# A scan's last group reordered on all engines, and one block of attention scores moved behind a tile of values

## The chip, the cores and the metric

The kernel runs on one core of a Trainium2 chip. A core has five engines with instruction streams of their own: TensorE (matmuls, called PE in the profile; its weight loads are PEld), VectorE (DVE), ScalarE (ACT), GpSimd (POOL) and SyncE (SP, which here only issues DMAs). They wait for one another by semaphores that are raised when an instruction ends. The metric is the device time of one launch in microseconds, lower is better.

## The reference, cut to what matters

The program is a two-layer network (convolution mixer, dilated attention and two SwiGLU layers) followed by a second two-layer network: a bidirectional state-space mixer (SSD) and a bidirectional gated linear attention mixer (GLA). All of it is float32, for 512 positions and 1024 channels. The change touches the end of the first and the start of the second of the last two:

```python
def ssd_scan(xh, dt, a, bm, cm):            # 4 chunks of 128 positions, 8 groups of 4 heads
    def step(state, inp):
        cum = jnp.cumsum(lac, axis=1)
        decay = jnp.exp(jnp.where(causal, cum[:, :, None] - cum[:, None], -jnp.inf))
        cb = jnp.einsum('blgn,bsgn->blsg', cc, bc)
        y = jnp.einsum('blsgr,bsgrp->blgrp', cb[..., None] * decay, xdt)      # within the chunk
        y = y + jnp.einsum('blgn,bgrpn->blgrp', cc, state) * jnp.exp(cum)[..., None]
...
def ssd_mixer(...):
    y = ssd_scan(forward) + rev(ssd_scan(backward)) + xh * d_skip
    y = y * silu(z)
    y = rmsnorm(y per group of 256 channels, gnorm)      # root of the mean square
    return y @ w_out                                     # 2048 x 1024
...
def gla_scan(q, k, v, lg):                   # 4 heads, chunks of 64
        qg = qc * jnp.exp(cum); kg = kc * jnp.exp(-cum)
        att = jnp.where(causal, jnp.einsum('blhk,bshk->bhls', qg, kg), 0.0)
        o = jnp.einsum('bhls,bshv->blhv', att, vc) + jnp.einsum('blhk,bhkv->blhv', qg, s)
```

## The kernel before, in words

Each large product is done as three passes of TensorE over split float32 numbers: high weights by high data, high weights by low data and low weights by high data. A unit is one block of weights, 128 x 2048 numbers. For each unit SyncE loads `raw`, ScalarE writes `whi` (L741), GpSimd (once, in the last group, VectorE) writes `wlo` (L652), and TensorE uses both. There are two buffers of each, taken in turn by even and odd units, so ScalarE may write the `whi` of unit n only when TensorE has marked the end of unit n-2: `high()` waits for `mm` to reach `2 * (n - 1)`, two marks for each unit.

The scan runs over eight groups of heads with four chunks each; chunk number n counts to 31, and the last group, 7, has n = 28 to 31. Nothing is planned at run time: the order on each engine is the order in which its code is written, and each waits at its own semaphores. For each n:

- ScalarE adds the bias of both directions to decay rows that a DMA brought (`biased`, L1046), VectorE takes the smaller of the two (`least`, L1705), and ScalarE takes the exponential (`exponential`, L1063).
- GpSimd multiplies the masked products of C and B with the step sizes, once for each direction (L680), adds the two (L683) and multiplies the sum with the exponential (L686). The result `MT` is the weight of the chunk.
- TensorE computes what the state carries in (L2537) and the chunk's own part (L2541): `chunk_out`.
- VectorE sums the parts (`collect`), and multiplies two chunks at a time with the gate (`gate`, L1745).

At the end of a group ScalarE sums squares (`squares`, L1085), VectorE scales the sum (L1696), ScalarE takes the root (L1089), VectorE inverts it and scales the whole group with it (L1698, L1700), and TensorE transposes the result (`turn_out`, L2519). ScalarE keeps it in `sY` (`turned_out`, L1094) and splits it into `sHi` (`y_hi`, L761), and VectorE makes `sLo` (`y_low`, L1750). These 16 tiles are the data of the output product (units 132 to 139, `U_SSD_OUT` and on).

In the last group TensorE fills its waits with the output product of the first two output tiles, k = 0 (unit 132) and k = 1 (unit 133): `out_high` (L2570), `out_low_weight` (L2575) and `out_low` (L2581). The tiles j = 0 to 13 of the data come from earlier groups; 14 and 15 are the last group's own. Only after j = 14 and 15 of k = 0 is unit 132 marked as done. Then the third output tile follows, unit 134, from L2641. ScalarE's order after the last group is: wait for the residual sum that VectorE makes from output tile 0 (L1435), write its high part and its square (L761, L772), and only then write the `whi` of unit 134:

```python
for i in range(4):
    for s in range(2):
        if i or s:
            ahead(U_SSD_OUT, i, s)
        split_square(5, 2 * i + s)
```

At the start of GLA, TensorE computes the values of head 0 in tiles of 128 positions (`projected`; a half of one tile is 12 matmuls of 512 columns). The scores of head 0 (`scores(0)`, L2721 and L2724) are placed between the two tiles of one call, and they wait until VectorE has multiplied queries and keys with their decays (L1906).

Of the kernel before, what the change touches and what calls it, by code (L numbers as in the profile page):

```python
# [14 lines left out]
P = 128  # L15
# [10 lines left out]
HPG = 4  # L26
# [158 lines left out]
def build(nc, A, out, stop=None):  # L185
# [8 lines left out]
    with ExitStack() as ctx:  # L194
# [5 lines left out]
        def S(name):  # L200
            if name not in sems:
                sems[name] = ctx.enter_context(nc.semaphore(name))
            return sems[name]
# [191 lines left out]
        def coupling(n):  # L395

            return m_ssd[("P0", "P1")[n % 2]][:, :]

        FB = bank[2]
        DTH = 2 * SSD_HEADS  # L400

# [224 lines left out]
        def _(pool):  # L626
# [43 lines left out]
            def coupled(n):  # L670

                g, c = n // NT, n % NT
                if c == 0:
                    pool.wait_ge(S("cb_ready"), 2 * g + 2)
                if n >= 2:
                    pool.wait_ge(S("mt_ready"), n - 1)
                if n:
                    pool.wait_ge(S("p_ready"), n)
                for d, dst in enumerate((coupling(n), acc[:, :])):
                    pool.tensor_tensor(v3(dst, HPG), bc(heads("dt", c, d, g), P), rep(m_ssd["CB"][:, SEQ * d + P * c:SEQ * d + P * (c + 1)], HPG),  # L680
                                       ALU.mult).then_inc(S("p_part"), 1)
                pool.wait_ge(S("p_part"), 2 * n + 2)
                pool.tensor_tensor(coupling(n), coupling(n), acc[:, :], ALU.add).then_inc(S("p_ready"), 1)  # L683
                pool.wait_ge(S("p_ready"), n + 1)
                pool.wait_ge(S("ex_ready"), n + 1)
                pool.tensor_tensor(weights(n), weights(n), coupling(n), ALU.mult).then_inc(S("mt_ready"), 1)  # L686
# [45 lines left out]
        def _(act):  # L732
# [236 lines left out]
            if on("ssd"):  # L969
# [179 lines left out]
                def last_group(g):  # L1149

                    for k in range(4):
                        y_hi(k)
                    exponential(NT * g)
                    biased(NT * g + 1)
                    turned_out(g - 1, 0)
                    exponential(NT * g + 1)
                    biased(NT * g + 2)
                    turned_out(g - 1, 1)
                    y_hi(4)
                    exponential(NT * g + 2)  # L1160
                    biased(NT * g + 3)
                    for k in range(5, 8):
                        y_hi(k)
                    exponential(NT * g + 3)
                    z_silu(g, 0)
                    z_silu(g, 1)
                    for k in range(8, 11):
                        y_hi(k)
                    unit_high(U_SSD_OUT + 1)
                    for k in range(11, 14):  # L1170
                        y_hi(k)
                    squares(g, 0)
                    squares(g, 1)
                    group_root(g)
                    for e in range(2):
                        turned_out(g, e)
                        y_hi(14 + e)
# [218 lines left out]
        def _(dve):  # L1396
# [224 lines left out]
            if on("ssd"):  # L1621
# [144 lines left out]
                def last_group(g):  # L1766
# [7 lines left out]
                    least(n + 1)  # L1774
                    keep_z(g)
                    y_low(0)
                    least(n + 2)
                    for k in range(1, 3):
                        y_low(k)
                    collect(g, 0)  # L1780
                    least(n + 3)
                    for k in range(3, 5):
                        y_low(k)
                    collect(g, 1)
# [1 line left out]
                    collect(g, 2)  # L1786
                    collect(g, 3)
                    gate(g, 1)
                    for k in range(5, 7):
                        y_low(k)  # L1790
                    normalise(g)
                    for k in range(7, IT):
                        y_low(k)

                def group(g):
# [256 lines left out]
        def _(pe):  # L2052
# [358 lines left out]
            if on("ssd"):  # L2411
# [172 lines left out]
                def last_group(g):  # L2584
# [9 lines left out]
                    chunk_out(g, 1)  # L2594
                    unit(U_SSD_OUT)
                    pe.wait_ge(S("sy_kept"), 2 * g)
                    for ks in (range(0, 4), range(4, 6)):
                        out_high(0, ks)
                        out_low_weight(0, ks)
                        if ks.start == 0:  # L2600
                            chunk_out(g, 2)
                    out_low(0, range(0, 4))
                    chunk_out(g, 3)
                    for ks in (range(6, 8), range(8, 14)):
                        out_high(0, ks)
                        out_low_weight(0, ks)
                    pe.wait_ge(w_hi, U_SSD_OUT + 2)
                    pe.wait_ge(S("ex_ready"), NT * SSD_GROUPS)
                    out_high(1, range(14))
                    for e in range(2):  # L2610
                        turn_out(g, e)
                    out_low(0, range(4, 14))
                    out_low(1, range(14))
                    for k in range(2):
                        if k:
                            unit(U_SSD_OUT + 1)
                            out_low_weight(1, range(14))
                        for j in range(14, IT):
                            out_high(k, (j,))
                            out_low_weight(k, (j,))  # L2620
                            mark(out_low(k, (j,)))
# [33 lines left out]
            if on("gla"):  # L2655
# [141 lines left out]
                gates(0)  # L2797
                projected("v", 0, 0, 0)
                projected("v", 0, 0, 1)
                projected("v", 0, 1, 0, lambda: scores(0))  # L2800
                projected("v", 0, 1, 1, lambda: keys(0))
                for h in range(GLA_HEADS):
                    head(h)
# [107 lines left out]
```

## Time and profile before

| | us |
|---|---|
| median of 3 runs | 2059.2 (2058.72 to 2060.91) |
| the profiled execution | 2057.88 |
| its span in the trace | 2055.9 |
| TensorE busy in the span | 2024.0 (98%) |
| VectorE, ScalarE, GpSimd busy | 896.8, 840.8, 1032.9 |

The profiled execution is 1.98 us longer than its span, which is what lies around the first and last instruction, and 1.3 us below the median. Busy times of TensorE are of pipelined matmuls: a record of one matmul of 512 columns is 0.39 us long, though the next starts 0.23 us after it. A row of a timeline gives start, duration, engine, line, operation, what it writes and reads, shape and count; in brackets stands how long the engine was idle before it and what ended that. "issue" means that the profile shows nothing for which the engine waited.

### The profile page before, as it was taken

To read this page: it belongs to the slowest core of one execution; us is meant where nothing else is said; L and a number is where in the kernel's file an instruction comes from. 1 tells how busy PE (TensorE), PEld (TensorE's weight loads), DVE (VectorE), ACT (ScalarE), POOL (GpSimd) and SP (SyncE) were. 2 spreads that over 40 slices of the span, in tenths; PEclk is the share of its full clock that TensorE was granted. 3 is DMA by queue.
4 is the path that set the end of the run, shared out by engine and by line. 5 is a ranking of instruction groups with operands and counts; after the bars stand their busy time and mean duration, and the time that the engine had idled before them with its cause. 6 is when DMAs were issued, how large, how long until landed. Compare 5 with 4: busy or idle time off the path is not lost.

```text
span 2055.9 us, 25781 instructions
## 1 busy us (share of the span) xinstructions
PE 2024.0 (98%) x9884; PEld 1654.1 (80%) x9884; DVE 896.8 (44%) x1411; ACT 840.8 (41%) x1341; POOL 1032.9 (50%) x855
## 2 busy tenths in 40 slices
PE   9999999999999999999999999999999999999998
PEld 7888888888877777888888778988887876677787
DVE  3184433322144435334322388778875215443331
ACT  4123222222244443222222377677774325544543
POOL 4455544545532224544545468788885441323242
PEclk9999999999999999999999999999999999999999
DMA  5223233223433312333233334434432321112131
GB/s 169 97 87 113 83 103 103 84 84 97 126 91 93 92 42 82 103 103 102 84 89 101 102 105 123 122 104 114 133 103 62 105 84 62 60 63 81 43 103 62
DMA packets 259365, 193.28 MB, mean 94 GB/s; under 512 B 9459, under 2 KB 247335, under 8 KB 259256
## 3 DMA queue, kind: packets, MB, share of 16 engines
q1 hardware_dynamic: 256188, 190.67, 30.9%
q8 instruction: 77, 1.26, 0.3%
q10 hardware_dynamic: 3068, 1.09, 0.2%
q14 instruction: 32, 0.26, 0.0%
HBM read 189.46 MB, written 2.27 MB: 93 GB/s over the span
## 4 chain that ended last, share of the span: by engine, by line
PE 38%; issue 35%; POOL 21%; DVE 2%; ACT 2%; DMA 1%; POOLq 0%; SPq 0%; ACTq 0%; DVEq 0%
POOL wlo L652 21%; PE bank L2058 11%; PE bank L2060 11%; PE bank L2059 11%; PE bank L2541 1%; PE bank L2537 1%; PE bank L2505 1%; DMA raw<-in_conv_w_in 0%; DVE xc L1668 0%; ACT whi L741 0%; DVE hLo L1971 0%; DMA rows<-cums 0%; PE bank L2519 0%; PE bank L2493 0%; PE bank L2477 0%
## 5 line engine op out<-in xcount | busy, mean ns | idle before, releaser
L652 POOL TENSOR_TENSOR wlo<-raw,whi 128x512 fp32r<-128x512 f32 (+1 forms) x664 | 842.4, 1299 | 942.7 <-ACT whi L741 942.7
L2058 PE MATMUL bank<-hHi,whi 128*128 128x512 f32 (+1 forms) x1392 | 548.4, 394 | 3.8 <-DVE qk L1554 1.5
L2060 PE MATMUL bank<-hHi,wlo 128*128 128x512 f32 (+1 forms) x1392 | 540.7, 388 | 0.0
L2059 PE MATMUL bank<-hLo,whi 128*128 128x512 f32 (+1 forms) x1392 | 540.4, 388 | 0.0
L741 ACT ACTIVATE whi<-raw 128x2048 fp32r<-128x2048 f32 (+1 forms) x167 | 301.8, 1807 | 476.0 <-PE bank L2060 473.0
L2058 PEld LDWEIGHTS bank<-hHi,whi 128*128 128x128 f32 x1392 | 261.4, 188 | 63.2 <-issue 6.6
L2060 PEld LDWEIGHTS bank<-hHi,wlo 128*128 128x128 f32 x1392 | 261.3, 188 | 54.8
L2059 PEld LDWEIGHTS bank<-hLo,whi 128*128 128x128 f32 x1392 | 261.5, 188 | 53.2 <-issue 1.2
L2058 PE MATMUL bank<-whi,hHi 128*128 128x256 f32 (+1 forms) x640 | 219.4, 343 | 2.2 <-POOL wlo L652 1.8
L2060 PE MATMUL bank<-whi,hLo 128*128 128x256 f32 (+1 forms) x640 | 208.5, 326 | 0.0
L2059 PE MATMUL bank<-wlo,hHi 128*128 128x256 f32 (+1 forms) x640 | 208.3, 326 | 0.0
L1435 DVE TENSOR_TENSOR xT<-xT,bank 128x512 f32<-128x512 f32 x47 | 32.3, 687 | 303.3 <-PE bank L2060 290.4
L2058 PEld LDWEIGHTS bank<-whi,hHi 128*128 128x128 f32 x640 | 121.6, 190 | 20.2 <-issue 8.2
L2059 PEld LDWEIGHTS bank<-wlo,hHi 128*128 128x128 f32 x640 | 121.7, 190 | 13.7 <-issue 4.5
L2060 PEld LDWEIGHTS bank<-whi,hLo 128*128 128x128 f32 x640 | 121.5, 190 | 10.4
L1668 DVE SCALAR_TENSOR_TENSOR xc<-bank,vecT,xc 128x510 f32<-128x510 f32 (+1 forms) x96 | 72.0, 749 | 3.7 <-ACT xc L987 0.3
L2060 PE MATMUL bank<-f0aHi,wlo 128*128 128x512 f32 x176 | 68.5, 389 | 0.0
L2060 PE MATMUL bank<-f1aHi,wlo 128*128 128x512 f32 x176 | 68.5, 389 | 0.0
L2058 PE MATMUL bank<-f0aHi,whi 128*128 128x512 f32 x176 | 68.5, 389 | 0.0
L2059 PE MATMUL bank<-f0aLo,whi 128*128 128x512 f32 x176 | 68.5, 389 | 0.0
L2058 PE MATMUL bank<-f1aHi,whi 128*128 128x512 f32 x176 | 68.5, 389 | 0.0
L2059 PE MATMUL bank<-f1aLo,whi 128*128 128x512 f32 x176 | 68.5, 389 | 0.0
(387 smaller groups left out, 2930.7 us busy)
## 6 DMA issues: line engine op xcount, KB each, us to landing
raw<-in_ssd_w_in SPq DMA_DIRECT2D x48, 512.0 KB, 4.8
raw<-in_ffn_w_gate SPq DMA_DIRECT2D x44, 512.0 KB, 4.7
raw<-in_ffn_w_up SPq DMA_DIRECT2D x44, 512.0 KB, 4.7
raw<-in_gla_w_in SPq DMA_DIRECT2D x40, 512.0 KB, 4.6
rows<-cums SPq DMA_DIRECT2D x64, 256.0 KB, 5.4
raw<-in_ffn_w_down SPq DMA_DIRECT2D x32, 384.0 KB, 3.6
raw<-in_attn_w_qkv SPq DMA_DIRECT2D x24, 512.0 KB, 4.5
raw<-in_conv_w_in SPq DMA_DIRECT2D x23, 512.0 KB, 4.4
```

Source lines behind the costliest of these rows:

```text
L652: ins = pool.tensor_tensor(wlo[s][:, part], raw[s][:, part], whi[s][:, part].bitcast(F32), ALU.subtract)
L741: act.activation(whi[s][:, 0:w], raw[s][:, 0:w], ACT.Copy).then_inc(w_hi, 1)
L1435: tt(x, x, bank[b][:, :], ALU.add).then_inc(res_done, 1)
L1668: ins = stt3(y[:, to:to + w], u[:, frm:frm + w], tapcol(j, ct), y[:, to:to + w], ALU.mult, ALU.add)
L2058: pe.matmul(dst, hi1, hi2, start=first, stop=False)
L2059: pe.matmul(dst, hi1, lo2, start=False, stop=False)
L2060: return pe.matmul(dst, lo1, hi2, start=False, stop=last)
L2505: ins = pe.matmul(bank[4 + step][:, 256 * d:256 * d + 256], bt[:, P * c:P * (c + 1)], xw_buf(step, d), start=True, stop=True)
L2537: pe.matmul(carried_bank(c, d), conv_tile(g, 3)[:, P * c:P * (c + 1)], m["stt"][:, SEQ * step + 256 * d:SEQ * step + 256 * d + 256], start ...
L2541: ins = pe.matmul(intra_bank(c)[:, 64 * h:64 * h + 64], weights(n)[:, P * h:P * (h + 1)], xt[:, 256 * c + 64 * h:256 * c + 64 * h + 64], s ...
```

## The change

`last_coupling(n)` names a buffer for n = 30 and 31 only. For these two chunks GpSimd no longer makes the product of the second direction; VectorE makes it, into `t32`, between `y_low(0)` and `least(30)`, and raises a semaphore that GpSimd waits for before its addition. The order of VectorE, ScalarE and TensorE in the last group changes as below. ScalarE gets one activation more, a square root of one column of ones ahead of the squares. In GLA the scores of head 0 stand behind both tiles of values rather than between them.

```diff
+        def last_coupling(n):
+            return t32[n % 2][:, :] if n >= NT * SSD_GROUPS - 2 else None
+        def coupled_aside(n):
+            return S("x_in3"), 16 + n - (NT * SSD_GROUPS - 3)
...                                   (GpSimd, coupled)
+                other = last_coupling(n)
                 for d, dst in enumerate((coupling(n), acc[:, :])):
+                    if d and other is not None:
+                        break
                     pool.tensor_tensor(v3(dst, HPG), ...
-                pool.wait_ge(S("p_part"), 2 * n + 2)
-                pool.tensor_tensor(coupling(n), coupling(n), acc[:, :], ALU.add).then_inc(S("p_ready"), 1)
+                if other is None:
+                    pool.wait_ge(S("p_part"), 2 * n + 2)
+                else:
+                    pool.wait_ge(S("p_part"), n + NT * SSD_GROUPS - 1)
+                    pool.wait_ge(*coupled_aside(n))
+                pool.tensor_tensor(coupling(n), coupling(n), acc[:, :] if other is None else other, ALU.add).then_inc(S("p_ready"), 1)
...                                   (ScalarE, last_group)
                     exponential(NT * g + 1)
+                    turned_out(g - 1, 1)
                     biased(NT * g + 2)
-                    turned_out(g - 1, 1)
                     y_hi(4)
...
                     exponential(NT * g + 3)
+                    for k in range(8, 11):
+                        y_hi(k)
                     z_silu(g, 0)
                     z_silu(g, 1)
-                    for k in range(8, 11):
+                    for k in range(11, 14):
                         y_hi(k)
                     unit_high(U_SSD_OUT + 1)
-                    for k in range(11, 14):
-                        y_hi(k)
+                    act.activation(m["hcol"][:, 2:3], ones[:, 0:1], ACT.Sqrt)
                     squares(g, 0)
...                                   (VectorE, last_group)
                     y_low(0)
+                    for c in (2, 3):
+                        tt(v3(last_coupling(n + c), HPG), bc(heads("dt", c, 1, g), P), rep(m["CB"][:, SEQ + P * c:SEQ + P * (c + 1)], HPG),
+                           ALU.mult).then_inc(coupled_aside(n + c)[0], 1)
                     least(n + 2)
                     for k in range(1, 3):
                         y_low(k)
+                    least(n + 3)
                     collect(g, 0)
-                    least(n + 3)
...
-                    for k in range(5, 7):
-                        y_low(k)
+                    y_low(5)
                     normalise(g)
-                    for k in range(7, IT):
+                    for k in range(6, IT):
                         y_low(k)
...                                   (TensorE, last_group)
-                    for ks in (range(0, 4), range(4, 6)):
-                        out_high(0, ks)
-                        out_low_weight(0, ks)
-                        if ks.start == 0:
-                            chunk_out(g, 2)
-                    out_low(0, range(0, 4))
+                    out_high(0, range(5))
+                    out_low_weight(0, range(5))
+                    chunk_out(g, 2)
+                    out_low(0, range(3))
+                    for j in range(5, 8):
+                        out_high(0, (j,))
+                        out_low_weight(0, (j,))
                     chunk_out(g, 3)
-                    for ks in (range(6, 8), range(8, 14)):
-                        out_high(0, ks)
-                        out_low_weight(0, ks)
+                    out_high(0, range(8, 14))
+                    out_low_weight(0, range(8, 14))
                     pe.wait_ge(w_hi, U_SSD_OUT + 2)
                     pe.wait_ge(S("ex_ready"), NT * SSD_GROUPS)
                     out_high(1, range(14))
                     for e in range(2):
                         turn_out(g, e)
-                    out_low(0, range(4, 14))
+                    unit(U_SSD_OUT + 1)
+                    out_low_weight(1, range(14))
+                    out_low(0, range(3, 14))
                     out_low(1, range(14))
                     for k in range(2):
-                        if k:
-                            unit(U_SSD_OUT + 1)
-                            out_low_weight(1, range(14))
                         for j in range(14, IT):
                             out_high(k, (j,))
                             out_low_weight(k, (j,))
...                                   (TensorE, GLA)
-                projected("v", 0, 1, 0, lambda: scores(0))
+                projected("v", 0, 1, 0)
+                scores(0)
                 projected("v", 0, 1, 1, lambda: keys(0))
```

## Rows read from the trace of the kernel before

**Rows 1.** The page, part 1: busy time, share and instructions.
```profile
PE 2024.0 (98%) x9884; PEld 1654.1 (80%) x9884; DVE 896.8 (44%) x1411; ACT 840.8 (41%) x1341; POOL 1032.9 (50%) x855
```
**Rows 2.** Waits of TensorE: total us, times, longest.
```profile
PE bank L2721 <- DVE kg L1906: 2.3, 1, 2.3
PE bank L2519 <- DVE szs L1700: 1.8, 1, 1.8
```
**Rows 3.** Timeline of TensorE, the scan's last group and the output product.
```profile
1538.73 2.04 PE L2570 MATMUL bank<-sHi,whi 128*128 128x512 f32 x4 [1.53 <-issue]
...
1542.06 1.03 PE L2537 MATMUL bank<-stt,xC 128*128 128x256 f32 x4
...
1558.83 1.09 PE L2519 MATMUL bank<-ident,szs 128*128 128x128 f32 x8 [1.76 <-DVE szs L1700]
1559.68 7.06 PE L2581 MATMUL bank<-sLo,whi 128*128 128x512 f32 x24
...
1567.94 3.33 PE L2575 MATMUL bank<-sHi,wlo 128*128 128x512 f32 x14
...
1572.47 0.39 PE L2641 MATMUL bank<-sHi,whi 128*128 128x512 f32 x1
```
**Rows 4.** Timelines of TensorE and VectorE around head 0's scores.
```profile
1704.21 0.39 PE L2060 MATMUL bank<-whi,hLo 128*128 128x512 f32 x1
1706.93 1.13 PE L2721 MATMUL bank<-gO,kg 128*128 128x128 f32 x8 [2.34 <-DVE kg L1906]
...
1706.10 0.69 DVE L1906 TENSOR_TENSOR kg<-gQK,kg 128x512 f32<-128x512 f32 x1
1710.41 0.42 DVE L1915 TENSOR_TENSOR diff<-diff,gdec 128x256 f32<-128x256 f32 x1 [3.62 <-PE bank L2724]
```
**Rows 5.** Timeline of ScalarE, the same stretch.
```profile
1535.62 1.28 ACT L1046 ACTIVATE rows<-rows,ncum 128x128 f32<-128x128 f32 x4 [2.40 <-DMA rows<-cums]
...
1543.64 0.60 ACT L1063 ACTIVATE MT<-bank 128x512 f32<-128x512 f32 x1
1544.26 1.28 ACT L1073 ACT_TABLE_LOAD   x1
1545.55 0.72 ACT L1073 ACTIVATE szs<-szs 128x256 f32<-128x256 f32 x2
...
1553.61 0.42 ACT L1085 ACTIVATE back<-szs 128x256 f32<-128x256 f32 x1 [0.75 <-DVE szs L1745]
...
1554.48 0.19 ACT L1085 ACTIVATION_READ_ACCUMULATOR back<-szs 128x1 f32 x1
...
1570.09 1.90 ACT L741 ACTIVATE whi<-raw 128x2048 fp32r<-128x2048 f32 x1
```
**Rows 6.** Timeline of VectorE, the same stretch.
```profile
1533.28 1.65 DVE L1750 TENSOR_TENSOR sLo<-sY,sHi 128x512 fp32r<-128x512 f32 x1
1538.06 0.70 DVE L1705 TENSOR_TENSOR bank<-bank,rows 128x512 f32<-128x512 f32 x1 [3.14 <-ACT bank L1046]
...
1553.50 3.48 DVE L1750 TENSOR_TENSOR sLo<-sY,sHi 128x512 fp32r<-128x512 f32 x2
1556.91 0.16 DVE L1696 TENSOR_SCALAR stat<-stat 128x4 f32<-128x4 f32 x1
...
1558.69 5.50 DVE L1750 TENSOR_TENSOR sLo<-sY,sHi 128x512 fp32r<-128x512 f32 x9
```
**Rows 7.** Timeline of GpSimd, the same stretch.
```profile
1542.49 1.03 POOL L680 TENSOR_TENSOR acc<-dt,CB 128x512 f32<-128x512 f32 x1
...
1550.50 5.93 POOL L652 TENSOR_TENSOR wlo<-raw,whi 128x512 fp32r<-128x512 f32 x4 [3.47 <-ACT whi L741]
1572.07 10.95 POOL L652 TENSOR_TENSOR wlo<-raw,whi 128x512 fp32r<-128x512 f32 x8 [15.63 <-ACT whi L741]
```
**Rows 8.** Windows: PE, PEld, DVE, ACT, POOL busy, granted clock, DMA.
```profile
1539.20:1539.70 0.50, 0.50 (x2) 0.33 (x2) 0.50 (x1) 0.50 (x2) 0.19 (x1) 0.50 1.09 315
...
1706.90:1708.00 1.10, 1.06 (x9) 0.98 (x9) 0.00 (x0) 0.00 (x0) 0.00 (x0) 1.00 0.00 0
```

## The prediction

> **What bounds the kernel now.** I read part 1 of the page first: TensorE is busy 2024.0 of 2055.9 us [rows 1], so all that this change can win is idle time or slowed matmuls of TensorE. The list of TensorE's waits then says where such time lies: the longest single ones are 2.3 us before the scores of head 0 and 1.8 us before the last group's transposes [rows 2]. The timeline of TensorE through the last group shows what surrounds these: a gap of 1.53 us before the first output matmuls (called "issue", but it ends with the `turned_out` of ScalarE), then the 1.76 us before the transposes, then 24 low passes that span 7.06 us, where 24 at full rate would span 5.6 (24 x 0.2265, and 0.16 by which a record outlasts its step) [rows 3]. The full rate is one matmul of 512 columns each 0.2265 us: from 1567.94 to 1572.47 there are 20 (14 of L2575, then six of k = 1) [rows 3]. Last I read the other engines' timelines to see which chain ends each of these waits. The sum below follows two points: T, the start of the last transposes (1558.83 before), and R, the start of the third output tile (1572.47 before) [rows 3]. What TensorE gains ahead of T is worth nothing by itself, as it waits there in any case.
>
> **The scores of head 0.** The last matmul before them starts at 1704.21, so the next could start at 1704.44; the scores start at 1706.93, and the cause, the last product of VectorE, ends at 1706.10 + 0.69 = 1706.79 [rows 4]. The loss is 2.49 us. Moved behind one half tile more (12 matmuls, 12 x 0.2265 = 2.72 us), the scores would start at 1707.16, which leaves 0.23 us to spare. The chain that ends at 1706.79 starts from gate products that are not moved. Behind the scores, the transposes of the keys now come 2.7 us after them rather than 5.4, and VectorE needs four products of 0.42 us in between [rows 4], about 1.7 us: still covered. ScalarE's `whi` of the next unit gets free earlier, not later. Gain: **2.5 us**, between 0 (if a new wait appears at once) and 2.5.
>
> **T, the last transposes.** Their chain is ScalarE's and VectorE's. It starts with decay rows that a DMA lands at 1535.6 [rows 5]; nothing in the change moves that load, since SyncE's order is the same and what it waits for (the exponentials of chunks 28 and 29) is not moved.
> - `turned_out(6, 1)` goes into the 2.40 us in which ScalarE waits for those rows [rows 5]. TensorE's gap of 1.53 us goes, but `y_hi(4)` becomes needed at once and is made only behind the eight bias activations that start at 1535.62, near 1538.6, so some 0.6 us stay. All this is ahead of T.
> - VectorE's two products go into its idle 3.14 us ahead of `least(30)` [rows 6]. The trace has no such product of two SBUF operands of this size in this spot. The neighbour `y_low(0)` took 1.65 us while GpSimd worked, and nine others took 5.50 us, 0.61 each, while it was idle [rows 6]. Two products are so 1.2 to 3.3 us; I take 3.2, by the neighbour. That ends at about 1538.1 and costs `least(30)` nothing to 0.2 us. GpSimd sheds two products of 1.03 us [rows 7], so the last two weights of chunks are ready sooner; ahead of T as well.
> - `exponential(31)` stood at 1543.64 behind `least(31)`, itself behind `collect(0)`. With `least(31)` first, ScalarE runs through: about 0.4 us earlier, 1543.2.
> - The silus' table load, four silus, six `y_hi` and the `whi` of unit 133 keep their total; only their order changes.
> - The new root brings a table load of 1.28 us and a 0.2 us activation ahead of the squares, +1.5 us. A table load costs no more than its length here: the one at 1544.26 was followed by a silu at 1545.55 [rows 5]. Against it, the squares waited 0.75 us for the gate and will no more [rows 5].
> The last sum of squares ended at 1554.48 + 0.19 = 1554.67 [rows 5]; now 1554.67 - 0.4 + 1.5 - 0.75 = 1555.0. Before, that was not the bound: VectorE was inside two `y_low` until 1556.98 [rows 6], and the table load ran beside it. With one `y_low` fewer it comes free near 1555.1. From L1696 to T it took 1558.83 - 1556.91 = 1.92 us [rows 3, 6], with GpSimd idle (it had ended at 1550.50 + 5.93 = 1556.43) [rows 7]. That gives T = 1557.0 at the least. But `whi` of unit 133 now ends at about 1551.5, a micro-second late against before (GpSimd started behind it at 1550.50), so GpSimd is in its four passes until about 1557.4, and the scaling of the group (L1700) falls into them. Beside GpSimd a `y_low` took 1.74 us instead of 0.61 [rows 6]: so up to 1.5 us more, one pass (5.93 / 4) [rows 7]. T lies in 1557.0 to 1558.6; I take 1557.8, the middle, since a pass is met at any point. TensorE reaches the place near 1555.1 and idles 2.7 us.
>
> The Trainium skill (SBUF — State Buffer, section "SBUF: two separate sides") has a rule for it: VectorE and GpSimd take a shared port pair as an exclusive lock for a whole instruction, and the loser blocks. The rows at 1.74 against 0.61 us agree. The Trainium skill (ScalarE: Activation LUTs, section "What ACT_TABLE_LOAD costs") speaks against the root ahead of the squares: it adds a drain of 1.38 us to each load. By that T would be 1.4 us later; the row at 1545.55 shows a start 0.01 us behind the load, so I go by the row.
>
> **From T to R.** Before: T to R took 13.64 us: the transposes 0.85, 50 matmuls at 0.2265 (11.3), and 1.5 lost to `y_low` [rows 3]. After, the 14 low-weight matmuls of k = 1 stand first, and one low pass more is left: 14 + 11 + 14 + 6 = 45 matmuls up to and with j = 15 of k = 0, then only six of k = 1. VectorE's ten `y_low` behind the scaling (0.61 each) are ahead of TensorE throughout, so the 1.5 us are won.
> But the third output tile needs the `whi` of unit 134, and that chain is short of cover now. Its buffer is unit 132's, free with the last matmul of k = 0. Behind this come VectorE's residual sum, ScalarE's high part and square, and then L741 at 1570.09 for 1.90 us, so 1571.99 [rows 5]. Counted from 1567.94, when the first matmul behind k = 0 started [rows 3], this is 4.05 us, and some 0.06 to TensorE: 4.11. Before, 20 matmuls (4.53 us) stood in between, so nothing waited, with 0.4 us to spare. Now there are six (1.36 us): TensorE idles 2.75 us. So R = T + 0.85 + 45 x 0.2265 + 4.11 = T + 15.15 = 1572.95, 0.5 us later than before. The bounds of T give -0.3 to +1.3 us.
> Further on, GpSimd makes the `wlo` of units 134 and 135 in 10.95 us from the end of `whi` [rows 7]; TensorE needs the second 48 matmuls (10.9 us) behind R. Before, ScalarE wrote `whi` 0.48 us ahead of R, now 0.06: up to 0.25 us of waiting. SSD in all: +0.75 us (-0.3 to +1.6).
>
> **TensorE's clock.** Once in this stretch it fell: behind the idle 1.53 us the granted clock is 0.50, the 1.2 GHz level [rows 8], and the eight matmuls from 1538.73 to 1542.06 took 3.33 us instead of 1.81 [rows 3], 1.5 us lost. Behind the idle 2.34 us at the scores it stayed 1.00 [rows 4, 8]. The change makes two idle stretches of 2.7 us at T and before R, longer than both, and TensorE sets the pace behind each. Cost: 0 to 3.0 us. I take 0, by the row nearest in length. The fall that goes with the old gap lay ahead of T and wins nothing.
>
> **Sum.** -2.5 + 0.5 + 0.25 = -1.75 us against the profiled 2057.88, so 2056.1; the median of the runs lies 1.3 above that execution, so I put it at 2059.2 - 1.75, about **2057.5**. That is 0.09% and, with less than about 0.2% (4.1 us) not to be told from no change here, "the same".
>
> **Rivals.**
> - *The clock falls behind one or both new idle stretches.* For it: they are longer than any in this region, and a shorter one already did it. Against: 2.34 us did not. One fall gives 2059.0, two give 2060.5, slower than before; it decides as soon as the two together cost more than 1.75 us. Chance 0.32.
> - *The third tile's weights are covered anyhow*, and the order on TensorE pays in full: R = T + 0.85 + 51 x 0.2265 = T + 12.4 = 1570.2, 2.3 us earlier, with the scores -4.8: 2054.4. Against: the wait on unit 132's marks stands in the code. Chance 0.09.
> - *VectorE's products do not fit into its idle time.* They would delay `least(30)`, and by ScalarE's unbroken chain T, by up to 1.5 us: 2058 to 2059. Against: 3.14 us of room. Chance 0.1.
> - *The scores' move does not do what it says*, as the wait comes back at the keys or the increments: 2.5 us less gain, 2060.0. Against: each needs less than it has. Chance 0.06.
> The forecast itself has 0.43, with a range of its own of 2056.3 to 2059.1. With all of them the range is 2055.0 to 2061.0. Faster by over 0.2% is the second rival and little else: 0.09. Slower needs two falls and a late T, or a part of this mechanism that I have not seen: 0.06. The same: 0.85.
>
> **What the profile of the changed kernel would show.** No wait at L2721. At L2570 no wait of 1.5 us. At L2519 a wait of 2 to 3 us for L1700, which ends 0 to 1.8 us earlier than before. At L2641 a new wait of about 2.7 us for L741: if it is not there, the forecast is wrong. L1696 would follow the squares at once, and the L2581 rows would run at 0.23 us each. Windows behind both waits tell by their granted clock whether the first rival holds. A time below 2055 or above 2061 would say that I have missed a chain.

## The result and the profile after

The changed kernel takes 2062.18 us (median of 20 runs, 2059.79 to 2066.46) against 2058.77 us before (20 runs): ratio 1.0014, 95% interval 1.0008 to 1.0020. It is slower by 0.14%. The forecast was 2057.5 us in a range of 2055.0 to 2061.0, so the time lies above the range, and the sign is the other one. The profiled execution took 2061.72 us, with a span of 2059.8 us.

First the longest waits of TensorE after the change (total us, times, longest; they answer to [rows 2]):

```profile
PE bank L2537 <- DVE szs L1716: 2.9, 1, 2.9
PE bank L2658 <- ACT whi L756: 2.6, 1, 2.6
...
PE bank L2749 <- DVE gO L1933: 1.8, 1, 1.8
PE bank L2588 <- ACT sHi L776: 1.8, 2, 1.3
```

Lines have shifted: L2537 is the last transposes (L2519 before), L2588, L2593 and L2599 are the output passes (L2570, L2575, L2581), L2658 is the third output tile (L2641), L2749 the transposes of the keys (L2732), L2738 the scores (L2721). On the other engines L1716, L1712 and L1933 are the scaling of the group, the step on its four sums and the span products, that is the products ahead of the keys' transposes (L1700, L1696, L1915); L756 and L660 write `whi` and `wlo` (L741, L652). The wait at the scores is gone, a new one of 1.8 us stands at the keys, the wait at T has grown, and the forecast wait of 2.6 us before the third tile is there.

TensorE's timeline, changed kernel, for [rows 3]:

```profile
1548.28 1.83 PE L2588 MATMUL bank<-sHi,whi 128*128 128x512 f32 x3 [1.26 <-ACT sHi L776]
1549.91 2.22 PE L2593 MATMUL bank<-sHi,wlo 128*128 128x512 f32 x6
1551.97 3.33 PE L2588 MATMUL bank<-sHi,whi 128*128 128x512 f32 x14
1558.24 1.97 PE L2537 MATMUL bank<-ident,szs 128*128 128x128 f32 x8 [2.94 <-DVE szs L1716]
1559.86 4.25 PE L2593 MATMUL bank<-sHi,wlo 128*128 128x512 f32 x14
1563.94 5.83 PE L2599 MATMUL bank<-sLo,whi 128*128 128x512 f32 x25
...
1575.06 0.65 PE L2658 MATMUL bank<-sHi,whi 128*128 128x512 f32 x1 [2.57 <-ACT whi L756]
1575.51 0.63 PE L2659 MATMUL bank<-sLo,whi 128*128 128x512 f32 x1
```

The 25 low passes span 5.83 us, which is the full rate: the 1.5 us that VectorE's `y_low` cost are won. But the eight transposes take 1.62 us to the next row instead of 0.85, the 14 passes behind them 4.08 instead of 3.17, and behind the third tile's wait matmuls start 0.43 us apart. The windows (PE, PEld, DVE, ACT, POOL busy, granted clock, DMA) show why, for [rows 8]:

```profile
1559.00:1560.00 1.00, 1.00 (x7) 1.00 (x5) 1.00 (x3) 0.61 (x1) 0.00 (x0) 0.50 1.01 304
...
1576.00:1577.00 1.00, 1.00 (x4) 0.81 (x3) 1.00 (x2) 1.00 (x2) 1.00 (x2) 0.50 0.00 0
```

The clock is at 0.50, the 1.2 GHz level, behind both idle stretches. VectorE's timeline, for [rows 6]:

```profile
1552.96 1.78 DVE L1766 TENSOR_TENSOR sLo<-sY,sHi 128x512 fp32r<-128x512 f32 x1
1554.69 1.21 DVE L1712 TENSOR_SCALAR stat<-stat 128x4 f32<-128x4 f32 x1
1556.18 0.18 DVE L1714 RECIPROCAL stat<-stat 128x4 f32<-128x4 f32 x1 [0.27 <-ACT stat L1104]
1556.39 1.79 DVE L1716 TENSOR_TENSOR szs<-szs,stat 128x1024 f32<-128x1024 f32 x1
```

and GpSimd's beside it, for [rows 7]:

```profile
1551.20 5.90 POOL L660 TENSOR_TENSOR wlo<-raw,whi 128x512 fp32r<-128x512 f32 x4 [6.10 <-ACT whi L756]
```

Even the step on four columns (L1712) takes 1.21 us instead of 0.16 while GpSimd is at its four passes, and the scaling 1.79 instead of 1.22. Last, the keys: TensorE, then VectorE, then GpSimd, and ScalarE ahead of it.

```profile
1711.47 1.05 PE L2738 MATMUL bank<-gO,kg 128*128 128x128 f32 x8
...
1719.61 1.09 PE L2749 MATMUL bank<-ident,diff 128*128 128x128 f32 x8 [1.84 <-DVE gO L1933]
```

```profile
1714.86 0.43 DVE L1933 TENSOR_TENSOR diff<-diff,gdec 128x256 f32<-128x256 f32 x1 [3.76 <-PE bank L2741]
1715.20 1.51 DVE L1933 TENSOR_TENSOR gO<-gO,gdec 128x256 f32<-128x256 f32 x1
1716.64 1.51 DVE L1933 TENSOR_TENSOR diff<-diff,gdec 128x256 f32<-128x256 f32 x1
1718.07 1.48 DVE L1933 TENSOR_TENSOR gO<-gO,gdec 128x256 f32<-128x256 f32 x1
```

```profile
1713.71 5.56 POOL L660 TENSOR_TENSOR wlo<-raw,whi 128x512 fp32r<-128x512 f32 x4 [13.41 <-ACT whi L756]
```

```profile
1711.73 1.91 ACT L756 ACTIVATE whi<-raw 128x2048 fp32r<-128x2048 f32 x1 [1.47 <-PE bank L2078]
```

The same two in the kernel before:

```profile
1713.41 1.92 ACT L741 ACTIVATE whi<-raw 128x2048 fp32r<-128x2048 f32 x1 [7.47 <-PE bank L2060]
1715.41 5.01 POOL L652 TENSOR_TENSOR wlo<-raw,whi 128x512 fp32r<-128x512 f32 x4 [19.41 <-ACT whi L741]
```

Three of the four span products, which took 0.42 us each [rows 4], now take 1.5 us. The 12 matmuls that now run ahead of the scores let ScalarE write its next `whi` earlier: it starts 0.26 us behind the start of the scores (1711.47), where it started 6.48 us behind it before (1706.93). With it GpSimd's low part now starts ahead of the span products; before, it began at 1715.41, when they had ended at 1711.8.

All profiles are put together by a few marks on TensorE: F, the first matmul of chunk 28; T; R; Q, the fourth output tile; S, the scores; G, the gate products of head 1 (the first such row behind S). Each column is a difference of two starts in a timeline, in us:

| kernel | F to T | T to R | R to Q | Q to G | S to G | G to end |
|---|---|---|---|---|---|---|
| before | 25.48 | 13.64 | 10.88 | 136.23 | 12.65 | 336.32 |
| changed | 25.33 | 16.82 | 12.60 | 135.72 | 11.91 | 336.42 |
| difference | -0.15 | +3.18 | +1.72 | -0.51 | | +0.10 |

With 0.44 us less ahead of F this makes 3.9 us, the difference of the spans. Each kernel has one profile, so these are differences of two single executions.

### The profile page after: what moved, and what is told of

The parts are those of the page before. It is cut to its first block, busy times and chain, and to the rows that moved or that the text cites. A ratio compares the mean times of both kernels' runs of the same rounds, so it can differ in the third digit from the quotient of the medians.

```text
span 2059.8 us, 25784 instructions
## 1 busy us (share of the span) xinstructions
PE 2025.8 (98%) x9884; PEld 1655.7 (80%) x9884; DVE 902.9 (44%) x1413; ACT 840.8 (41%) x1342; POOL 1031.5 (50%) x853
## 3 DMA queue, kind: packets, MB, share of 16 engines
q8 instruction: 77, 1.26, 0.3%
## 4 chain that ended last, share of the span: by engine, by line
PE 38%; issue 35%; POOL 21%; ACT 2%; DVE 2%; DMA 1%; POOLq 0%; SPq 0%; ACTq 0%; DVEq 0%
POOL wlo L660 21%; PE bank L2076 11%; PE bank L2078 11%; PE bank L2077 11%; PE bank L2559 1%; PE bank L2555 1%; PE bank L2523 1%; DMA raw<-in_conv_w_in 0%; DVE xc L1684 0%; ACT whi L756 0%; DVE hLo L1989 0%; DMA rows<-cums 0%; ACT sHi L776 0%; PE bank L2537 0%; PE bank L2511 0%
## 5 line engine op out<-in xcount | busy, mean ns | idle before, releaser
L660 POOL TENSOR_TENSOR wlo<-raw,whi 128x512 fp32r<-128x512 f32 (+1 forms) x664 | 842.7, 1300 | 947.1 <-ACT whi L756 947.1
L756 ACT ACTIVATE whi<-raw 128x2048 fp32r<-128x2048 f32 (+1 forms) x167 | 301.7, 1807 | 469.8 <-PE bank L2078 466.9
```

What stands on the lines that cost most here:

```text
L660: ins = pool.tensor_tensor(wlo[s][:, part], raw[s][:, part], whi[s][:, part].bitcast(F32), ALU.subtract)
L756: act.activation(whi[s][:, 0:w], raw[s][:, 0:w], ACT.Copy).then_inc(w_hi, 1)
```

## The experiments

Each was timed in five rounds beside the kernel before on the same chip; medians and ratios are against those runs. Where two kernels of this list are compared in time, it is by their ratios to the kernel before. Each has one profile.

**1. The scores' move alone.**
```diff
-                projected("v", 0, 1, 0, lambda: scores(0))
+                projected("v", 0, 1, 0)
+                scores(0)
```


> The kernel before with the scores of head 0 moved behind both tiles of values, nothing else. Theory A (the earlier release of the weights lets GpSimd's low parts run beside VectorE's four span products, which then take 1.5 us each instead of 0.42, so the keys wait about 1.8 us): the wait at the scores (2.3 us) goes, one of 1.8 us comes at the keys, and the time falls by 0.5 us only. Theory B (the move pays in full and what the changed kernel shows there is a result of its other edits): 2.5 us less.

Measured: 2057.15 us against 2059.8, ratio 0.9991 (0.9982 to 1.0000). S to G is 11.91 us, Q to G 135.72, exactly as in the changed kernel, and the waits of TensorE have

```profile
PE bank L2732 <- DVE gO L1915: 1.8, 1, 1.8
```

So the wait at the keys comes with the move, not with the other edits. In the profile it wins 0.51 us; the runs show 1.9 us, with an interval that holds both. Two profiles of kernels with the old order (experiments 2 and 4) can explain the rest: there the clock fell behind the scores' wait and S to G was 14.18 us, not 12.65. Against those two the move wins 2.1 us from Q to G. How often the kernel before meets this was not measured.

**2. The tail alone.** The kernel before, with the low-weight passes of k = 1 moved.
```diff
+                    unit(U_SSD_OUT + 1)
+                    out_low_weight(1, range(14))
                     out_low(0, range(4, 14))
...
-                        if k:
-                            unit(U_SSD_OUT + 1)
-                            out_low_weight(1, range(14))
```


> The kernel before with one edit: the 14 low-weight passes of k = 1 stand right behind the last transposes rather than between k = 0 and k = 1. Theory A (the third output tile's high weights lose their cover): TensorE idles about 2.7 us before it, R moves from T + 13.6 to T + 15.15, so 1.5 us slower, and 3.1 us slower if the clock falls behind the idle time. Theory B (the loss of the changed kernel comes from the scan's chain on ScalarE and VectorE, not from the tail): no slower than before, or 1.4 us faster because the low passes no longer wait for VectorE.

Measured: 2062.29 us against 2059.8, ratio 1.0012 (1.0003 to 1.0021). T to R is 15.05 us with the clock at full rate throughout. The forecast's formula gives 14.93 here, since this kernel has one low pass less behind T than the changed one (44 matmuls, not 45). This one reordering is by itself as slow as the whole change, though in this profile no clock fell behind R.

```profile
PE bank L2640 <- ACT whi L741: 2.6, 1, 2.6
```

**3. The changed kernel with the old tail.**
```diff
-                    unit(U_SSD_OUT + 1)
-                    out_low_weight(1, range(14))
...
+                        if k:
+                            unit(U_SSD_OUT + 1)
+                            out_low_weight(1, range(14))
```


> The changed kernel with its tail put back (the low-weight passes of k = 1 again between k = 0 and k = 1). Theory A: no wait for the third tile's high weights (2.6 us) and no slowed clock behind it (1.6 us); the low passes wait for VectorE again for up to 1.5 us: 3 to 4.4 us faster than the changed kernel, so about the time of before or 1 us below. Theory B: at most 1 us from the changed kernel.

Measured: 2058.25 us against 2059.8, ratio 0.9993 (0.9984 to 1.0002), so 4.3 us below the changed kernel's 1.0014. No wait at the third tile, R to Q 10.88. T to R is 15.33, as the clock still fell behind T. TensorE idled 3.6 us there, longer than in the changed kernel, since its clock had stayed up ahead of T in this execution and it came earlier:

```profile
1558.75 1.97 PE L2537 MATMUL bank<-ident,szs 128*128 128x128 f32 x8 [3.65 <-DVE szs L1716]
```

**4. The changed kernel with the old place of the scores.**
```diff
-                projected("v", 0, 1, 0)
-                scores(0)
+                projected("v", 0, 1, 0, lambda: scores(0))
```


> The changed kernel with the scores of head 0 put back between the two tiles. Theory A: the 1.8 us at the keys go and the 2.3 us at the scores come back, 0.5 us slower than the changed kernel. Theory B (the move pays in full): 2.5 us slower.

Measured: 2062.87 us against 2059.8, ratio 1.0017 (1.0008 to 1.0026): 0.6 us above the changed kernel's ratio, less than the intervals can tell. In this execution the clock stayed up behind T, and T to R is 15.26: the changed kernel's 16.82 less one fall. The idle time at T was shorter too, as the clock had been at 0.50 ahead of T and TensorE came later:

```profile
1558.79 1.09 PE L2537 MATMUL bank<-ident,szs 128*128 128x128 f32 x8 [1.61 <-DVE szs L1716]
```

**5. The idle stretches filled.** Both got 11 matmuls into an unread bank.
```diff
                     out_high(1, range(14))
+                    pe.wait_ge(S("sz_ready"), NT * SSD_GROUPS)
+                    for j in range(11):
+                        pe.matmul(bank[1][:, :], m_ssd2["sHi"][:, P * j:P * (j + 1)], tile(m_ssd2["sHi"], 0), start=True, stop=True)
...                                 (and the same ahead of the wait for unit 134's high weights)
```


> The changed kernel with 11 matmuls of 512 columns more in each of its two new idle stretches (ahead of the last transposes and ahead of the third output tile), into a bank that nothing reads. They add 2 x 2.5 us of work to TensorE and no use. Theory A (behind the idle stretches the clock falls to half, and that is a part of the loss): T to R is 15.1 to 15.3 us and R to the fourth tile 10.9 us in every execution, as the clock stays at 1.00, and the time is 1.5 to 3 us below the changed kernel in spite of the added work. Theory B (the slow clock is not tied to the idle time): not faster than the changed kernel, or slower.

Measured: 2059.2 us against 2059.43, ratio 0.9998 (0.9989 to 1.0007): 3.3 us below the changed kernel with 5 us of useless work more. The two intervals do not overlap. T to R is 15.23 and R to Q 11.01, and no window from T to Q is below 1.00:

```profile
1562.00:1566.00 4.00, 4.00 (x21) 3.35 (x20) 4.00 (x7) 2.54 (x4) 0.00 (x0) 1.00 0.84 245
...
1577.00:1580.00 3.00, 3.00 (x15) 2.45 (x14) 2.72 (x2) 2.58 (x3) 3.00 (x3) 1.00 0.00 0
```

So theory A holds: the clock was lost to the idle time. The work put in costs nothing, as it fits into time in which TensorE waited. In the changed kernel's profile the slow clock cost 3.4 us behind 5.5 us of idle time.

**6. The third tile's weights first.**
```diff
+                ahead(U_SSD_OUT, 0, 1)
                 for i in range(4):
                     for s in range(2):
-                        if i or s:
+                        if i:
                             ahead(U_SSD_OUT, i, s)
                         split_square(5, 2 * i + s)
```


> The changed kernel, but ScalarE writes the high weights of the third output tile's unit before the high part and square of the residual rather than behind them. Theory A (the wait at R is for exactly this chain: residual sum, high part, square, weights): the weights come about 2.0 us earlier, the wait at the third tile shrinks from 2.6 to about 0.7 us, no fall of the clock behind it; 2 to 3.5 us faster than the changed kernel, about the time of before. Theory B (something else paces this place): within 0.5 us of the changed kernel.

Measured: 2059.52 us against 2059.43, ratio 0.9997 (0.9988 to 1.0006), 3.5 us below the changed kernel. The wait at the third tile is 0.7 us, and behind it the clock stayed up. T to R is 15.04 with one fall behind T. The fourth tile now waits 0.3 us for GpSimd (R to Q 11.48): the next link of the chain shows.

**7. The scores' move, with the weights behind the keys.**
```diff
-                value_piece(0, 1, 0)
                 turned_keys(0)
+                value_piece(0, 1, 0)
                 value_piece(0, 1, 1)
```


> The kernel before with the scores of head 0 behind both tiles, and ScalarE's high weights of the unit that follows placed behind its two copies of the turned keys, so that GpSimd's low parts don't run beside VectorE's span products. Theory A (the keys wait because both run at once): the span products take 0.42 us each, no wait at the keys, 2 us faster than with the move alone (2.5 us below before, 4 where the clock used to fall behind the scores' wait). Theory B (the span products are slow for another reason): still 1.5 us each, same time as the move alone.

Measured: 2055.57 us against 2059.43, ratio 0.9985 (0.9976 to 0.9994). VectorE's timeline has the span products at their old length, and there is no wait at the keys; S to G is 10.29 us, 1.62 less than with the move alone. The runs show 1.2 us less than with the move alone, with intervals that overlap.

```profile
1710.45 0.42 DVE L1915 TENSOR_TENSOR gO<-gO,gdec 128x256 f32<-128x256 f32 x1
1710.79 0.42 DVE L1915 TENSOR_TENSOR diff<-diff,gdec 128x256 f32<-128x256 f32 x1
1711.12 0.42 DVE L1915 TENSOR_TENSOR gO<-gO,gdec 128x256 f32<-128x256 f32 x1
```

**8. A first attempt at all of it.** The old tail, edits 6 and 7, and GpSimd held back:
```diff
                     pool.wait_ge(w_lo, U_SSD_OUT + 1)
+                    pool.wait_ge(S("sy_scaled"), SSD_GROUPS)
                     unit_low(U_SSD_OUT + 1)
```


> The changed kernel with four edits: the old tail on TensorE, the third tile's high weights ahead of the residual's high part, the GLA weights behind the turned keys, and GpSimd's low part of unit 133 held until VectorE has scaled the last group. Theory A: no wait at the third tile, the scaling of the group takes 1.2 us and L1712 0.2 us, T 1.5 us earlier than in the changed kernel, no wait at the keys: 5 us below before (2.5 from the scores, 2 to 3 from T). Theory B (T is paced by ScalarE's chain and the tail does not matter): 2.5 us below before.

Measured: 2061.69 us against 2059.43, ratio 1.0009 (1.0000 to 1.0018): a miss. T came 1.75 us earlier than in the changed kernel (F to T 23.58), as expected. But GpSimd's passes now ran beside the ten `y_low`, on which the old tail waits:

```profile
1557.56 1.22 DVE L1718 TENSOR_TENSOR szs<-szs,stat 128x1024 f32<-128x1024 f32 x1
1558.70 10.43 DVE L1768 TENSOR_TENSOR sLo<-sY,sHi 128x512 fp32r<-128x512 f32 x10
```

```profile
1558.91 6.66 POOL L660 TENSOR_TENSOR wlo<-raw,whi 128x512 fp32r<-128x512 f32 x4 [11.58 <-DVE szs L1718]
```

Ten took 10.43 us instead of 6.10. TensorE waited for them four times, 3.5 us in all, its clock fell to 0.50 among these waits, and T to R became 19.53. The contention had only been moved. For T the edit is the cleanest of all, since ahead of it nothing else differs from the changed kernel: the step on the four sums took 0.17 us and the scaling 1.22.

**9. Without the root ahead of the squares.**
```diff
-                    act.activation(m["hcol"][:, 2:3], ones[:, 0:1], ACT.Sqrt)
```


> The changed kernel without the square root ahead of the squares, so that the table load falls behind them again. Theory A (what sets the start of L1712 is VectorE's y_low beside GpSimd, and a table load behind the squares hides beside it): the last transposes start within 0.3 us of where they are in the changed kernel (25.3 us behind the first chunk), and the time is the changed kernel's within 0.5 us. Theory B (the root on ScalarE's chain costs its 1.5 us): T comes 1 to 1.5 us earlier. Theory C (it pays, as the root's load was on the path behind the squares): T comes 1.3 us later.

Measured: 2061.91 us against 2059.72, ratio 1.0010 (1.0001 to 1.0019). F to T is 25.17 against 25.33, as theory A has it. The root's place decides nothing that the runs can tell.

**10. The couplings back on GpSimd.**
```diff
-            return t32[n % 2][:, :] if n >= NT * SSD_GROUPS - 2 else None
+            return None
...
-                    for c in (2, 3):
-                        tt(v3(last_coupling(n + c), HPG), ...
```


> The changed kernel with both directions' couplings of chunks 30 and 31 on GpSimd again. Theory A (the couplings are ahead of T and off its path): the weights of chunk 31 come about 1.7 us later and TensorE waits longer at them, yet T moves by 0.3 us at most, and the time is the changed kernel's within 0.5 us. Theory B (VectorE's two products pay): 1 to 2 us slower. Theory C (they cost, by delaying least(30) and so ScalarE's chain): 0.5 us or more faster.

Measured: 2063.5 us against 2059.72, ratio 1.0024 (1.0014 to 1.0035). F to T is 24.94, 0.4 us *earlier*, and the waits at the chunks' weights rose from 1.4 to 3.2 us, as expected. The time is 2.1 us above the changed kernel's by the ratios (0.4 by the differences of the medians), beyond the 0.5 expected, though the intervals overlap. In this execution TensorE idled 3.6 us at T, its clock was at 0.50 from 1556.6 to 1563.6, and T to R was 17.99. As in experiment 3, the clock had stayed up ahead of T, so that TensorE came early and waited longer. The marks speak for theory A, the time for theory B; whether VectorE's two products pay is left open.

**11. The weights of unit 133 early.** The old tail, edit 7, and:
```diff
                     turned_out(g - 1, 1)
+                    unit_high(U_SSD_OUT + 1)
                     biased(NT * g + 2)
...
-                    unit_high(U_SSD_OUT + 1)
```


> The changed kernel with the old tail on TensorE, the GLA weights behind the turned keys, and ScalarE's high weights of unit 133 written in the 1.9 us in which ScalarE waits for the decay rows of chunk 30, rather than ahead of the squares. GpSimd's low part of unit 133 is then done by about 1551, before the last group's scaling. Theory A (port sharing with GpSimd and the 1.9 us on ScalarE delay T): L1712 and L1716 take 0.2 and 1.2 us, T comes 1.5 to 2.2 us earlier (23.3 us behind the first chunk), T to R is 13.7 to 14 us; 4 to 5 us below before. Theory B (T is paced by the chunks' chain up to the gate): T moves by less than 0.5 us, 2.5 us below before.

Measured: 2055.22 us against 2059.72, ratio 0.9980 (0.9971 to 0.9989). ScalarE's 1.9 us fit into its wait for the DMA, GpSimd was done by 1550.85, and F to T fell to 23.80. T to R is 13.78. The step on the sums and the scaling are short again:

```profile
1554.07 0.17 DVE L1712 TENSOR_SCALAR stat<-stat 128x4 f32<-128x4 f32 x1 [0.52 <-ACT back L1100]
1554.51 0.18 DVE L1714 RECIPROCAL stat<-stat 128x4 f32<-128x4 f32 x1 [0.27 <-ACT stat L1104]
1554.72 1.22 DVE L1716 TENSOR_TENSOR szs<-szs,stat 128x1024 f32<-128x1024 f32 x1
```

The scaling ended at 1555.94, and the transposes began 0.53 us later without a wait: here TensorE itself, on a clock at 0.50 up to 1554.3, sets T.

**12. And the tail split.** As 11, with edit 6 and half of the low-weight passes on each side.
```diff
+                    unit(U_SSD_OUT + 1)
+                    out_low_weight(1, range(7))
                     out_low(0, range(3, 14))
...
                         if k:
-                            unit(U_SSD_OUT + 1)
-                            out_low_weight(1, range(14))
+                            out_low_weight(1, range(7, 14))
```


> As weights_early, but half of the low-weight passes of k = 1 stand behind the last transposes and half between k = 0 and k = 1, and the third tile's high weights are written ahead of the residual's high part. Theory A: the seven passes in front cover VectorE's y_low (1.5 us won), the seven behind and the earlier weights cover the third tile; T to R falls to 12.5 us, 5 to 6 us below before. Theory B (one of the two covers is too short, or the fourth tile's low part comes late as ScalarE's order is changed): T to R is 13 us or more, or R to the fourth tile 11.5 us rather than 10.9; no better than weights_early.

Measured: 2053.96 us against 2059.72, ratio 0.9972 (0.9962 to 0.9982), the fastest of all, though its interval overlaps with that of experiment 11. F to T 23.20, T to R 12.65, R to Q 10.88, S to G 10.29; no wait of TensorE above 1.9 us is left in the span but the one at its start.

## Why the prediction was wrong, step by step

Two steps failed, each by more than the whole gain that was forecast: the clock (3.4 us) and the scores (2.0 us). T came 0.9 us later than forecast besides.

- **From T to R: right in its mechanism and its size.** The wait for unit 134's high weights is there (2.57 us from the end of the last record, 2.73 counted as the forecast counts it, forecast 2.75). Where the clock stayed up, T to R was 15.26 us in experiments 4 and 9 against 15.15. It cost more than I took it for only by what follows it.
- **TensorE's clock: the step that failed by most.** I took 0 of "0 to 3.0 us", "by the row nearest in length". It fell behind both idle stretches in the profiled execution: 1.68 us in T to R (0.77 at the transposes and 0.91 at the next 14 passes), 1.72 in R to Q. Experiment 5 shows that it is the idle time that does it. The first rival had this mechanism with 0.32; it was the likeliest. The row that I leaned on (2.34 us idle, clock 1.00) was one draw: in both later profiles that have this wait (experiments 2 and 4) the window from 1700 to 1720 us is at 0.91. It also came from an execution with a mean clock of 0.999, while the 33 of the kernel before beside experiments 1 to 4 were at 0.995 to 0.998. This mean does not tell the two kernels apart (the changed one's 20 are at 0.994 to 0.997), so the clock's share rests on the profiles and on experiment 5. The idle stretches at these places in all profiles:

| idle time of TensorE | profiles that have it | clock fell to 0.50 behind it |
|---|---|---|
| 2.82 to 3.65 us, at T | changed, 3, 6, 10 | in all four |
| 2.57 or 2.58 us, at R | changed, 2, 4, 9, 10 | in all but 2 |
| 2.34 or 2.35 us, at the scores | before, 2, 4 | in 2 and 4 |
| 1.61 to 2.24 us, at T | before, 2, 4, 7, 9 | in none |
| 1.84 us, at the keys | changed, 1, 3, 5, 6, 9, 10 | in none |

The length alone does not decide it: ahead of T the clock fell at shorter waits too, in experiment 7 behind 1.87 us, in the changed kernel within a wait of 1.26 us.

The Trainium skill (TensorE: Matmul & The Clock Gate, Part 1) says of the rise to the full clock that its point varies from run to run. The profiles agree for the fall: the changed kernel and experiments 3, 4, 6 and 9 run the same matmuls up to T, and ahead of T the clock fell 15.0, 14.4, 15.2 and 16.8 us behind F in the changed kernel, 4, 6 and 9 (by windows of 0.2 us), and not at all in 3. The longer it was down there, the later TensorE came and the shorter it idled at T (1.61 us in 4, 3.65 in 3).

- **The scores: the wait removed, another put in its place.** This step failed as well. The gain was 0.51 us in the profile where I had 2.5. I had seen that ScalarE's weights "get free earlier, not later", and counted it as harmless. But the earlier `whi` sets GpSimd off beside four products of VectorE that stand right before the keys, and three of them take 1.5 us instead of 0.42. Experiment 7 takes this away and finds 2.13 of the 2.5 us (Q to G is 134.10 against 136.23); 0.38 us are a new wait for `gv` ahead of G. My own text names, further on, the port lock of the Trainium skill (SBUF — State Buffer, section "SBUF: two separate sides") for T, and GpSimd's passes from 1713.71 to 1719.27 lie beside the three slow products; I did not ask there what the scores' move would trigger. The fourth rival had named a wait that comes back at the keys, with a chance of 0.06, but by "each needs less than it has", not by GpSimd.
- **The rivals were counted as if only one could hold.** The first and the fourth came together. By the forecast's own prices, two falls (2060.5) and the scores' gain lost (2.5) are 2063.0, beyond the upper end of the range, and so is what it named itself as slower, two falls and a late T (2061.3). At the lower end the second rival's 2054.4 was outside too.
- **T: mis-sized.** Forecast 1.0 us earlier against F (1557.8 against 1558.83), measured 0.15; on the clock of the profile before this is 1558.68, just past the bound of 1558.6. The chain was the right one, yet I let only the scaling meet GpSimd. The step on four columns met it as well, 1.21 us instead of 0.16, and the scaling took 0.57 us more. Experiment 8 confirms the cause: with GpSimd held back and nothing else changed ahead of T, both are short and T comes 1.75 us earlier. In experiment 11 it is 1.5 us, but there ScalarE's order differs too.
- **VectorE's couplings and the root: right in size.** The two products took 3.20 us as forecast, in the gap; neither edit moves T by more than 0.4 us (9, 10). The drain that the Trainium skill (ScalarE: Activation LUTs, section "What ACT_TABLE_LOAD costs") adds to each table load is not there in this trace, as I had forecast: the load at 1551.08 ended at 1552.36, and the root started at 1552.37.
- **The fourth tile's 0.25 us** did not show. In the changed kernel the slowed TensorE hid it. In experiment 2 TensorE had no wait there either: GpSimd's eight passes ended at 1584.58, 0.06 us ahead of Q. The 0.13 us that R to Q is longer there also stand in experiment 5, where GpSimd is no bound: the first matmuls behind a wait start 0.34 us apart, not 0.23.

Put in the forecast's terms, the measured table reads -0.15 (T) + 1.50 (T to R) + 1.68 + 1.72 (clock) - 0.51 (scores) + 0.10 (rest) = +4.3 us behind F, near the 3.9 of the spans and the 3.4 of the medians. The forecast had -1.75.

## What to carry to other kernels

Before moving work to an earlier place on the busiest engine, count what it leaves as cover where it stood: here 20 matmuls had hidden a chain of 4.1 us (free buffer, residual, split, weights) with 0.4 us to spare, and the move left six. When an edit lets a buffer go earlier, follow who starts on it: an earlier start of GpSimd beside short VectorE operations took back 1.6 of the 2.1 us that the move could win. Price an idle stretch of TensorE of 2.5 us or more with the half clock behind it: here eight of nine such stretches had it. And when two rivals can hold at once, add their prices before you close the range.

## What the runs showed of the hardware that I had not expected

- An operation of VectorE on 128 x 4 numbers took 1.21 us instead of 0.16 beside GpSimd. It ended at 1555.90, and the pass of GpSimd that was under way when it started (1554.69) ended at 1555.89. In experiments 9 and 10 it took 1.25 and 1.19 us.
- Adding 22 useless matmuls (5 us of TensorE) to the changed kernel made it about 3 us faster, as they kept the clock at 2.4 GHz.
- The clock also fell where TensorE was not idle for long: in experiment 11 the windows 1700 to 1720 and 1720 to 1740 were at 0.95 and 0.96, though TensorE's longest wait there was 0.38 us, and G to the end took 338.07 us instead of 336.4. So did experiment 12 (0.94, 0.98 and 338.08 us), and experiment 7, with the same wait, did not (336.39 us). Why was not tried.
